# A two-layer hybrid encoder step on one core: the padding ids of the weight units, the order of the first norm, and two small transposes are moved

## The reference

```python
for l in range(DEPTH):                                   # DEPTH = 2
    h = rms_norm(x, w_norm1[l])
    a, gc, gb, q, k, v, u, vg = split(h @ w_in[l])       # 3x256, 512, 2x128, 2x256 columns
    z, conv_state = short_conv(gc * a, cache_conv[l], w_conv[l])     # y = gb * z
    q, k = partial_rope(q), partial_rope(k)
    y_attn = window_attention_with_sinks(q, k, v, cache_k[l], cache_v[l])
    y_gmlp = gelu(u) * (w_spatial[l] @ layer_norm(gelu(vg)) + b_spatial[l])
    mix = concat(rms_norm(gb * z), rms_norm(y_attn), rms_norm(y_gmlp))
    x = x + mix @ w_out[l]
    x = x + square(relu(rms_norm(x, w_norm2[l]) @ w_ff1[l])) @ w_ff2[l]
y = rms_norm(x, w_norm_final)
```

## Time and profile before

| | us |
|---|---|
| median of 3 runs | 2392.47 (2389.87 to 2393.46) |
| the profiled execution | 2393.46 |
| its span | 2391.6 |
| PE busy | 2313.5 (97%) |
| DVE busy | 1275.7 (53%) |
| ACT busy | 817.0 (34%) |
| POOL busy | 123.1 (5%) |
| mean granted PE clock | 0.986 of full |

### The profile page before, as it was taken

One profiled execution on the slowest core, in us unless ns is written; L12 is line 12 of the kernel. 1 busy time (PEld: TensorE's weight loads), 2 busy tenths in 40 slices (PEclk: granted clock), 3 DMA queues, 4 the chain that ended last, 5 costly groups with the idle time before them and its releaser, 6 DMA issues. The chain is left out here.

```text
span 2391.6 us, 32181 instructions
## 1 busy us (share of the span) xinstructions
PE 2313.5 (97%) x12710; PEld 2059.9 (86%) x12710; DVE 1275.7 (53%) x2205; ACT 817.0 (34%) x1697; POOL 123.1 (5%) x223
## 2 busy tenths in 40 slices
PE   7998999999999989999999999999999998999997
PEld 7987878999999968888898877789999997788885
DVE  5236865443343465765752578563343343766766
ACT  4123522454444422122231234134444443221222
POOL 4010000000000000000130100010000000000001
PEclk9999999999999999999999999999999999999999
DMA  5011001355455686656230110114555557666463
GB/s 177 27 32 44 19 32 43 106 199 215 176 217 198 236 305 255 223 199 246 97 70 27 36 40 19 45 36 161 192 210 208 180 193 302 255 237 263 176 235 118
DMA packets 190374, 361.67 MB, mean 151 GB/s; under 512 B 13308, under 2 KB 96800, under 8 KB 190224
## 3 DMA queue, kind: packets, MB, share of 16 engines
q1 hardware_dynamic: 186368, 352.33, 40.5%
q0 software_dynamic: 2704, 3.10, 0.6%
q10 hardware_dynamic: 1152, 4.19, 0.5%
HBM read 228.01 MB, written 131.37 MB: 150 GB/s over the span
## 5 line engine op out<-in xcount | busy, mean ns | idle before, releaser
L1507 PE MATMUL ps<-hT_hi,w_hi 128*128 128x384 f32 x1824 | 615.2, 337 | 2.7 <-DVE x L1171 2.7
L1509 PE MATMUL ps<-hT_hi,w_lo 128*128 128x384 f32 x1824 | 613.3, 336 | 0.0
L1508 PE MATMUL ps<-hT_lo,w_hi 128*128 128x384 f32 x1824 | 613.3, 336 | 0.0
L1507 PE MATMUL ps<-w_hi,ring 128*128 128x512 f32 x896 | 353.1, 394 | 8.7 <-DVE w_lo L1274 7.5
L1508 PE MATMUL ps<-w_lo,ring 128*128 128x512 f32 x896 | 354.8, 396 | 0.0
L1509 PE MATMUL ps<-w_hi,ring 128*128 128x512 f32 x896 | 352.2, 393 | 0.0
L1507 PEld LDWEIGHTS ps<-hT_hi,w_hi 128*128 128x128 f32 x1824 | 343.4, 188 | 3.2 <-DVE x L1171 3.1
L1508 PEld LDWEIGHTS ps<-hT_lo,w_hi 128*128 128x128 f32 x1824 | 343.3, 188 | 0.0
L1509 PEld LDWEIGHTS ps<-hT_hi,w_lo 128*128 128x128 f32 x1824 | 343.2, 188 | 0.0
L1016 DVE TENSOR_TENSOR w_lo<-w_raw,w_hi 128x512 fp32r<-128x512 f32 (+1 forms) x232 | 143.4, 667 | 342.6 <-ACT w_hi L679 342.5
L1507 PE MATMUL ps<-w_hi,hT_hi 128*128 128x512 f32 (+1 forms) x720 | 279.5, 388 | 5.9 <-ACT vn L867 4.5
(11 more groups left out here) (205 smaller groups left out, 2685.1 us busy)
## 6 DMA issues: line engine op xcount, KB each, us to landing
ff_ops<-row_op SPq DMA_DIRECT2D x224, 512.0 KB, 3.9
ring<-ff_ops SPq DMA_DIRECT2D x56, 2048.0 KB, 8.0
w_raw<-in_w_ff SPq DMA_DIRECT2D x128, 256.0 KB
b<-in_w_ff SPq DMA_DIRECT2D x24, 1024.0 KB, 14.4
w_raw<-in_w_in SPq DMA_DIRECT2D x56, 256.0 KB
w_raw<-in_w_out SPq DMA_DIRECT2D x32, 256.0 KB
ff_last<-last_op SPq DMA_DIRECT2D x32, 256.0 KB, 4.2
w_raw<-in_w_ff SPq DMA_DIRECT2D x8, 1024.0 KB, 10.1
```

The lines of the kernel that those rows point to most:

```text
L1507: pe.matmul(out, sh, mh, start=first, stop=False)
L1508: pe.matmul(out, sh, ml, start=False, stop=False)
L1509: return pe.matmul(out, sl, mh, start=False, stop=last)
```

## The change

Three things are moved; no instruction is added or removed.

1. The padding ids become 12 to 15 instead of 28 to 31. KVU gets the ids 16 to 23 (before 12 to 19), vg 24 to 31 (before 20 to 27), q keeps 32 to 39. So the eight KVU units and the eight vg units use the slots 0 to 7 in this order, where before they used 4 to 7 and then 0 to 3. On DVE, the low parts of the eight KVU units now stand in one row behind the taps of the second convolution group.
2. In norm 1, DVE's loop is written in another form: `normalise(t)`, the addition for t, then the split and `norm_low` for t-1.
3. On PE, the two transposes of `ccin` with their wait for `mid_in` stand ahead of column block 1 instead of behind its first row group.

```diff
-U_CONV, U_KVU, U_VG, U_Q, U_OUT, U_FF, U_END = 0, 12, 20, 32, 40, 56, 120
-PAD_IDS = range(28, 32)
+U_CONV, U_KVU, U_VG, U_Q, U_OUT, U_FF, U_END = 0, 16, 24, 32, 40, 56, 120
+PAD_IDS = range(12, 16)
...
# ACT, convolution
-                split(range(U_KVU, U_KVU + 4))
-                split(range(U_KVU + 4, U_KVU + 8))
+                split(range(U_KVU, U_KVU + 8))
...
# DVE, norm 1
-                normalise(1, 0)
-                for t in range(T):
-                    if t + 1 < T:
-                        normalise(1, t + 1)
+                for t in range(T + 1):
+                    if t < T:
+                        normalise(1, t)
                     if l > 0 and t < HALF:
                         now["l"] = l - 1
                         add_pair(STAGES - 1, t)
                         now["l"] = l
-                    split(first_splits(t))
-                    norm_low(1, t)
+                    if t >= 1:
+                        split(first_splits(t - 1))
+                        norm_low(1, t - 1)
                 split(range(4, 8))
...
# DVE, convolution
                 conv_gate(0)
-                split(range(U_KVU, U_KVU + 4))
                 conv_z(1)
                 conv_taps(1)
-                split(range(U_KVU + 4, U_KVU + 8))
+                split(range(U_KVU, U_KVU + 8))
                 conv_gate(1)
...
# PE, convolution
+                pe.wait_ge(*mid_in.at("last"))
+                pe.nop(nofuse=True)
+                for c in range(2):
+                    ins = pe.transpose(ps[:, 7, 16 * c:16 * c + 16], ccin[0:16, c * P:(c + 1) * P], ident[0:16, 0:16])
+                ins.then_inc(*cc_T.tick())
                 for cb in range(1, 6):
                     for g in range(GROUPS):
                         conv_cols(cb, g)
-                        if cb == 1 and g == 0:
-                            pe.wait_ge(*mid_in.at("last"))
-                            pe.nop(nofuse=True)
-                            for c in range(2):
-                                ins = pe.transpose(ps[:, 7, 16 * c:16 * c + 16], ccin[0:16, c * P:(c + 1) * P],
-                                                   ident[0:16, 0:16])
-                            ins.then_inc(*cc_T.tick())
```

## The result

The changed kernel takes 2409.54 us (median of 5 runs, 2406.03 to 2411.61), the kernel before 2392.47 (now of 5 runs, 2387.29 to 2397.24): a ratio of 1.0075, 95% interval 1.0058 to 1.0091. That is +17 us, and slower by more than 0.2%. Forecast were 2408.5 us and +16.0.

A forecast was written before the change was run, and what follows sets the result against it. PE, busy 2313.5 of 2391.6 us, was taken as the bound. Waits 3.4 + 4.1 + 3.1 + 1.2 = 11.8 us plus 4.2 of clock made 16.0, so 2408.5 us against the median of 2392.47; range 2400.5 to 2415.

The forecast's parts named there:

- First-layer transposes: PE in the first layer, at the moved `ccin` transposes: idle until the last `kc` transfers land, 3.4 us more than before.
- The bound of 4.1: First-layer `ccin` transposes: upper size of PE's added wait, if the release is no sooner than the transposes' old start.
- Second-layer transposes: PE in the second layer, at the moved `ccin` transposes: waits for `kc` slowed by POOL's loads alongside, 4.1 us taken.
- The branch that I named for it, 2.9: Second-layer `ccin` transposes: were SP's and POOL's loads apart, `kc` would land in 3.8 us, giving 2.9 us.
- Norm 1: DVE in the second layer's norm 1: idles for PE's products and never catches up, 3.1 us; first layer 0.
- The list of DVE's steps: Second layer's norm 1: DVE's norms, additions and low halves followed in time, with idle times of 2.3, 0.5 and 0.55 us.
- the lower bound of 2.4: Second layer's norm 1: 2.4 us if the release is quicker and PE's spare 0.2 us per step count; upper bound 3.4.
- Eighth KVU unit: End of the convolution, both layers: its load lands late after 2.4 us, PE waits 0.6 us twice, 1.2 us (0.6 to 3.4).
- The estimate of 2.6 us: Load of KVU's eighth unit: time by the skill's fixed 2.0 us and 436 GB/s; the term would be 1.6 us.
- Entry of q: PE's wait for the Gelu of `vn`: slots freed sooner bring nothing, as ACT waited for DVE; 2.25 us stays, gain 0.
- Clock: PE at half clock behind new gaps: 3.4 us for both `ccin` waits, 0.8 in norm 1; 4.2 us, bounds 0 and 7.

The follow-up runs named there:

- second profile: The changed kernel run once more, unaltered: median 2406.11 us, ratio 1.0068 to the kernel before; profiled execution 2418.37 us.

## Why the prediction was right, and where its terms were not

The path was named rightly: PE's idle time and clock, in the three places. Sum 16.0 us; measured 17 and 15 by the medians of the two sets of runs, 18 and 16 by their ratios, 14.7 and 17.7 by paced spans.

- **First-layer transposes: 3.4 forecast, 4.0 to 5.0 measured** (idle 3.95 alone, 4.63 and 4.89 in the whole; the profile counts it from the listed end of the product, 0.16 us behind the end of its slot, so 0.16 is added, and the 0.1 that was lost before taken off: 4.0, 4.7, 5.0). In the changed kernel SP's last issue came at 40.5 us instead of 40.0, as one of its issues took 1.3 us, and PE was ready at 40.11 instead of 40.46. The bound of 4.1 was too low, since I let the times of one execution stand for all.
- **Second-layer transposes: 4.1 forecast.** Alone it was 3.42 less the 0.28 idle before, so 3.1; in the whole change 2.00 and 1.69 less 0.28, so 1.7 and 1.4. This is the step that failed: "ACT's sum of squares of the ninth tile, and with it POOL's loads, is late too, so they stay side by side". POOL's first of these loads was issued 0.6 us later in its layer, SP's 2.7 us, and `kc` landed in 2.8 to 4.0 us instead of 4.9 to 6.0. The branch that I named for it, 2.9, was also too high, as it took the first layer's landing, which POOL's two loads slow as well.
- **Norm 1: 3.1 forecast, 2.4 measured** by the norm order alone and 2.7 in the whole. The list of DVE's steps came out within 0.1 us for each idle time (2.3, 0.5, 0.55 forecast; 2.19, 0.61, 0.59), the lower bound of 2.4 was the closer one.
- **Eighth KVU unit: 1.2 forecast, 2.7 in the whole, 2.6 alone.** The mechanism was right, the load's landing mis-sized: 3.2 us with the release, near the 3.5 of the larger row and not near the smaller. The estimate of 2.6 us from the Trainium skill ("DMA: Bandwidth & Descriptors", "Anatomy of one DMA — SWDGE (gpsimd) path") was too short as well; that section's figures are of transfers that GpSimd issues, and this load is issued by SP.
- **Entry of q: 0 forecast, 0 measured.** The waits stayed at 2.26 us.
- **Clock: 4.2 forecast, 3.4 measured** in the first profile, 1.7 behind each `ccin` stall and nothing in norm 1; in the second profile the clock was at half level for 6.8 us around the end of the first stall, 6.1 of them behind it, so 4.8 us were lost in all. That is 1.4 of the 3.0 us that its paced span has more.

So 3.4 + 4.1 + 3.1 + 1.2 + 4.2 became, in the changed kernel's first profile, 4.7 + 1.7 + 2.7 + 2.7 + 3.4 = 15.2, beside 14.7 paced, and in its second 5.0 + 1.4 + 2.8 + 3.1 + 4.8 = 17.1, beside 17.7. In the first, two terms were 1.3 and 1.5 us too low, one was 2.4 too high, two 0.4 and 0.8. That they cancelled is luck: the places and the kind of cost were named rightly, the total was better than its parts.

## What to carry to other kernels

A wait for a shared count of transfers costs what the last of them lacks, though the data that the instruction reads came first; give that data a semaphore of its own before moving the instruction ahead. When an edit delays one of two queues, look up what releases the other before you assume that they stay together. Where units share rotating slots, follow the chain to the last load: what counts is which unit the last-freed slot belongs to.

## What the runs showed of the hardware

**Two paces of the same products at full clock.** In each feed-forward stretch, a 128x384 product starts on the mean every 0.1733 or every 0.1767 us, with PE full and the granted clock 1.00. Of 26 such stretches in the 13 profiles (two layers each) 19 were fast and 7 slow, which makes up to 14.6 us between two executions, as much as the whole change costs. What sets the pace stays open; the changed kernel had both.

**The clock behind a gap.** Of PE's gaps ahead of the `ccin` transposes, behind those of 1.48, 1.56, 1.85 and 2.74 us the granted clock stayed at 1.00; behind those of 1.69, 2.00, 2.54, 3.42, 3.95 and 4.63 us it was at half level for 3.4 us, with those of 3.83 and 4.89 for 6.8 us, of which the first 1.6 and 0.7 us lay still in the gap. 2.95 us in norm 1 were followed by 1.00 each time. So all gaps over 3 us were paid for with 1.7 us or more, and below that the length alone does not decide: the smallest with a fall is 1.69, the largest without 2.95. What decides is not shown. The Trainium skill ("TensorE: Matmul & The Clock Gate", "Why this matters for your kernels") warns of idle gaps between bursts of products. For the five gaps over 3 us the traces agree, all were followed by a fall; of the seven shorter ones at these transposes three were, and of those in norm 1 none.
